# Moving the input rows and the two buffers of the normalised operand by 96 bytes within SBUF, in a two-block transformer layer

## The chip, the cores and the metric

The kernel runs on one core of one Trainium2 chip. The metric is the device time of one execution, in microseconds. Before the change three runs gave a median of 949.74 us (949.6 to 950.62).

## The reference

Two blocks of a layer model, one after the other, on 256 tokens of width 1024, all in float32:

```
h = rmsnorm(x, norm_mix)                               # norm 0
proj = h @ w_in                                        # state space, 3 attentions, gates
...
x = x + sum_i(sigmoid(gate_i) * (y_i @ w_branch_i)) @ w_out
h = rmsnorm(x, norm_ffn)                               # norm 1
x = x + (silu(h @ w_gate) * (h @ w_up)) @ w_down       # width 2816
x = rmsnorm(x, norm_final)
u = rms(x, ln_mix)                                     # norm 2
p = u @ w_in_2                                         # RWKV, latent attention, gated delta rule
...
x = x + y @ w_out_2
u = rms(x, ln_ffn)                                     # norm 3
x = x + relu(u @ w_ff1)**2 @ w_ff2                     # width 4096
```

## The kernel before

All weights stream from HBM through a ring of three slots of 16 KB per partition (`weights0` to `weights2`), in chunks of mostly 128 x 4096 values, fetched by SP's queue.

Products with the large weights are made with three matmuls in place of one. Each weight piece of 2048 columns is split into two parts: ScalarE copies it to a rounded part (`W_HIGH`, L1685), and VectorE subtracts that from the original (`W_LOW`, L2260). The other operand is split in the same way. `product3` (L680 to L688) then issues, for each tile of 128 rows of the contraction, high x high, high x low and low x high into the same accumulator. Its matmul is L686, and it is the line of most of TensorE's work. Every matmul has a weight load of its own: 128 columns of the stationary operand are loaded while the matmul before it streams its moving operand.

Two shapes occur at L686:

- 256 moving columns: the weight piece is stationary (`W_HIGH`, `W_LOW`), and the normalised operand, transposed, moves, all 256 tokens of it. The projections in of the first block read it from `FIRST_HIGH` and `FIRST_LOW` (over `BIAS`), those of the second block from `IN2_HIGH` and `IN2_LOW` (in `ARENA`), and both feed-forward parts, `ffn1` (11 chunks) and `ffn2` (8 chunks), from `OVER_HT` and `OVER_HN`. These two are names over the buffers `HT` and `HN`. A chunk is two jobs of `f_job_split` (L690), and a job two outputs of 8 x 3 matmuls: 11 x 2 x 2 x 24 = 1056 for `ffn1` and 8 x 2 x 2 x 24 = 768 for `ffn2`.
- 512 moving columns: the weights move and the operand is stationary (`t_half`, L710, the branch products and both `down` products). The stationary operand is mostly in `ARENA` or `BIAS`, for `out1` and a part of `out2` it is `OVER_HT` or `OVER_HN`. The last pieces of the `down` products and one piece of `branch` lie in `HT` and `HN` as moving weights.

Some chunks of `in2` are not split: L643 multiplies `HT` (moving) by the ring slot (stationary) in plain float32.

All engines' programs are written out by hand, each with its waits on semaphores. Places in SBUF come from the order of the allocations at the head of `build` (L239 to L258). `sb` takes the next free place, `placed` does so and also keeps it (they all begin on multiples of 32 bytes), and `over` lays a second name on a kept place. Sizes per partition: `X`, `HN` and `HT` 8192 bytes each, `STAT` 256, `RELB` 64 (on 32 partitions), `PICK0` 32, three ring slots of 16384, `BIAS` 16384, then `ARENA` with 104448. The offsets within `ARENA` of the pieces and of `IN2_HIGH`, `HID1_HIGH` and the like are multiples of 128 values, which is 512 bytes, and so are the steps between the tiles in them. So the modulo 512 of `ARENA`'s address is that of the ring slots, of `BIAS` and of all operands in them. There are two exceptions. `KEY_HIGH` and `KEY_LOW`, the second piece of the first `in2` chunk, have rows of 160 values, so that each further tile of the contraction starts 640 bytes on, 128 more modulo 512. `PICK0` and `PICK1` are tiny selectors, of which one column is repeated over all columns of an operand.

Of the kernel before, what the change touches and what calls it, by code (L numbers as in the profile page):

```python
# [20 lines left out]
ACT = mybir.ActivationFunctionType  # L21
AX_X = mybir.AxisListType.X

P = 128
# [5 lines left out]
NH = 8  # L30
# [183 lines left out]
def build(nc, x, weights, params, params2, consts, tables, rel_bias, norm_final, positions, table_dram, out):  # L214
    with ExitStack() as ctx:
        def sb(name, shape, dt=F32):
            return ctx.enter_context(nc.sbuf_tensor(name, shape, dt))
# [3 lines left out]
        def sem(name):  # L221

            if name not in sems:
                sems[name] = ctx.enter_context(nc.semaphore(name))
            return sems[name]
# [4 lines left out]
        def placed(name, shape):  # L230

            places[name] = (nc.sbuf_base + 31) // 32 * 32
            return sb(name, shape)

        def over(name, place, at, shape):

            return nc.alloc_sbuf_tensor_at(name, [P] + shape, F32R, offset=places[place] + 4 * at)

        X = sb("X", [P, TT, D])  # L239
        HN = placed("HN", [P, TT, D])  # L240
        HT = placed("HT", [P, KD, S])
        STAT = sb("STAT", [P, 64])
        RELB = sb("RELB", [32, 2 * NH])
        PICK = [placed("PICK0", [P, NH])]
        rings = [placed(f"weights{i}", [P, SLOT]) for i in range(NRING)]
        RING_LOW = [over(f"RING_LOW{i}", f"weights{i}", 0, [SLOT]) for i in range(NRING)]
        BIAS = placed("BIAS", [P, 16, S])
# [6 lines left out]
        PRM = sb("PRM", [P, NP1])  # L254
        PICK.append(placed("PICK1", [P, NH]))
        PICK = [over(f"PICK_PARTS{i}", f"PICK{i}", 0, [NH]) for i in range(2)]
        POS = sb("POS", [P, TT], I32)
# [59 lines left out]
        def tbl(name):  # L317
            a, b = TCOL[name]
            return TBL[:, a:b]
# [210 lines left out]
        def _(sp):  # L530
# [23 lines left out]
            for b in range(3):  # L554
                wait_fill_out(sp, ("down2", b))
                tt, dc = divmod(b, 2)
                sp.dma_start(out[0, tt * P:(tt + 1) * P, dc * 512:(dc + 1) * 512],
                             X[:, tt, dc * 512:(dc + 1) * 512]).then_inc(sem("out_stored"), 16)
            for j in range(2):
# [4 lines left out]
                cols = slice(512 + j * S, 512 + (j + 1) * S)  # L564
                sp.dma_start(out[0, P:S, cols], X[:, 1, cols]).then_inc(sem("out_stored"), 16)
            sp.wait_ge(sem("out_stored"), 16 * 5)
# [24 lines left out]
        def _(pe):  # L591
# [10 lines left out]
            def open_fill(name):  # L602
                f = state["fill"]
                assert FILLS[f][0] == name, (FILLS[f], name)
                b = FILLS[f][1]
                if FILL_USES[f]:
                    pe.wait_ge(sem(f"fill_out{b}"), FILL_USES[f])
                return BK[b]
# [9 lines left out]
            def close_fill(ins):  # L618
                state["fill"] += 1
                ins.then_inc(sem("fills_written"), 1)  # L620
# [154 lines left out]
            o = open_fill(("table",))  # L775
            close_fill(pe.matmul(o[0:2 * NH, 0:384], RELB[:, :], tbl("onehot")[0:32, :], start=True, stop=True))

# [33 lines left out]
            def both_parts(h, n, sign):  # L811

                return PICK[0 if sign > 0 else 1][:, h:h + 1].to_broadcast([P, n])

# [725 lines left out]
            def x_transposes(dc):  # L1540
# [3 lines left out]
                for b in (2 * dc, 2 * dc + 1):  # L1544
                    o = open_fill(("norm", 3, b))
                    for j in range(2):
                        for tt in range(TT):
                            k = 2 * b + j
                            ins = pe.transpose(o[:, j * S + tt * P:j * S + (tt + 1) * P],
                                               X[:, tt, k * P:(k + 1) * P], ident)  # L1550
                    close_fill(ins)
# [57 lines left out]
        def _(act):  # L1609
            for tt in range(TT):  # L1610
                act.dma_start(X[:, tt, :], x[0, tt * P:(tt + 1) * P, :]).then_inc(sem(f"x{tt}_in"), 16)
            act.dma_start(CST[:, 0:P], consts[:, 0:P]).then_inc(sem("params_in"), 16)
            act.dma_start(PRM[:, :], params).then_inc(sem("params_in"), 16)
            act.dma_start(TBL[0:32, :], tables).then_inc(sem("consts_in"), 16)
            act.dma_start(RELB[:, :], rel_bias).then_inc(sem("consts_in"), 16)
            act.dma_start(CST[:, P:NC], consts[:, P:NC]).then_inc(sem("consts_in"), 16)
# [9 lines left out]
            def half_squares(m, tt, dc):  # L1626
# [7 lines left out]
                else:  # L1634
                    wait_job_out(act, ("out1" if m == 1 else "out2", dc, tt))
                    junk = JUNK[m][:, 2 * tt + dc, :]
                cols = slice(dc * 512, (dc + 1) * 512)
                act.activation(junk, X[:, tt, cols], ACT.Square, accum_out=HALF_SUMS[:, 0, tt, dc:dc + 1])\
                    .then_inc(sem("half_sums"), 1)
# [567 lines left out]
        def _(dve):  # L2207
            steps = [0]

            def link(ins):  # L2210

                steps[0] += 1
                ins.then_inc(sem("dve_steps"), 1)
                dve.wait_ge(sem("dve_steps"), steps[0])
# [113 lines left out]
            link(dve.tensor_scalar(negident[:, :], ident, -1.0, None, ALU.mult))  # L2328
            dve.tensor_tensor(PICK[0][:, :], ident[:, 0:NH], ident[:, 32:32 + NH], ALU.add)
            dve.tensor_tensor(PICK[1][:, :], negident[:, 0:NH], negident[:, 32:32 + NH], ALU.add)  # L2330
            for tt in range(TT):
# [996 lines left out]
```

## Time and profile before

| | |
|---|---|
| median of 3 runs | 949.74 us (949.6 to 950.62) |
| profiled execution, its own time | 949.99 us |
| its span, first to last instruction | 948.4 us |
| TensorE busy, share of the span | 929.5 us, 98% |
| VectorE, ScalarE, GpSimd busy | 589.2, 470.8, 62.5 us |
| mean granted TensorE clock | 0.997 |
| moved by DMA | 149.86 MB |

The profiled execution took 0.25 us more than the median; its span leaves out 1.6 us around the instructions. A busy TensorE is not a TensorE at its peak, since matmuls overlap: a duration of one is not the time that it costs. What it costs is the distance from its start to the next one's start, called its interval below, and it is had from a stretch without waits, as time between the first and the last start divided by the number of matmuls less one.

### The profile page before, as it was taken

What the parts mean: (1) busy time and instruction counts of PE and PEld (TensorE: products, weight loads), DVE (VectorE), ACT (ScalarE), POOL (GpSimd) and SP (SyncE); (2) the same over time, 40 slices, a digit from 0 to 9 for tenths busy, and PEclk for the clock granted to TensorE, in tenths of its full rate; (3) what the DMA queues carried; (4) which work ended last, traced back from release to release, by engine and by line L of the source; (5) the groups of instructions that cost most, each with busy time, mean ns of one, the idle gap of its engine ahead of it and who ended that gap; (6) DMA issues with size and microseconds to landing.
All of it is one profiled execution on the core that took longest, in us unless ns stands there. A gap on an engine that the chain in (4) does not pass through costs nothing.

```text
span 948.4 us, 16840 instructions
## 1 busy us (share of the span) xinstructions
PE 929.5 (98%) x7117; PEld 825.9 (87%) x7117; DVE 589.2 (62%) x932; ACT 470.8 (50%) x707; POOL 62.5 (7%) x78
## 2 busy tenths in 40 slices
PE   6999999999999999999999999999999999999998
PEld 6999987787778789999988789888988799998886
DVE  5885445556678755555554669678867566655434
ACT  5654335555874454444443684556436454554331
POOL 1000000021003200000000000002450000000000
PEclk9999999999999999999999999999999999999999
DMA  9995552243446524445554442222000444555521
GB/s 349 205 375 192 189 189 89 90 167 131 164 188 250 191 107 178 178 178 188 189 200 162 178 148 100 89 90 90 3 2 18 163 178 178 189 188 205 214 94 45
DMA packets 14922, 149.86 MB, mean 158 GB/s; under 512 B 1712, under 2 KB 4144, under 8 KB 6272
## 3 DMA queue, kind: packets, MB, share of 16 engines
q1 hardware_dynamic: 12592, 139.65, 39.5%
q0 software_dynamic: 1296, 5.24, 3.0%
q10 hardware_dynamic: 960, 3.90, 1.1%
q8 instruction: 57, 0.93, 0.4%
q14 instruction: 17, 0.14, 0.0%
HBM read 144.59 MB, written 4.19 MB: 157 GB/s over the span
## 4 chain that ended last, share of the span: by engine, by line
PE 87%; DVE 5%; ACT 4%; issue 2%; POOL 1%; DMA 0%; ACTq 0%; DVEq 0%; POOLq 0%
PE bank L686 66%; PE bank L643 4%; PE bank L1423 3%; DVE W_LOW L2260 1%; PE bank L834 1%; POOL HN L3144 1%; PE bank L875 1%; PE bank L912 1%; ACT W_HIGH L1685 1%; PE bank L668 1%; PE bank L652 1%; PE bank L1290 1%; DMA PRM<-params_dram 0%; DVE OUT_LOW L2260 0%; DVE X L2567 0%
## 5 line engine op out<-in xcount | busy, mean ns | idle before, releaser
L2260 DVE TENSOR_TENSOR W_LOW<-weights,W_HIGH 128x2048 fp32r<-128x2048 f32 (+1 forms) x98 | 224.5, 2292 | 208.3 <-ACT W_HIGH L1685 208.2
L1685 ACT ACTIVATE W_HIGH<-weights 128x2048 fp32r<-128x2048 f32 (+1 forms) x98 | 186.7, 1907 | 257.0 <-PE bank L686 257.0
L686 PE MATMUL bank<-OVER_HT,W_HIGH 128*128 128x256 f32 x608 | 171.2, 282 | 0.2 <-DVE OVER_HN L2272 0.2
L686 PE MATMUL bank<-OVER_HT,W_LOW 128*128 128x256 f32 x608 | 170.7, 281 | 0.0
L686 PE MATMUL bank<-OVER_HN,W_HIGH 128*128 128x256 f32 x608 | 170.7, 281 | 0.0
L686 PEld LDWEIGHTS bank<-OVER_HT,W_HIGH 128*128 128x128 f32 x608 | 114.7, 189 | 0.8 <-issue 0.6
L686 PEld LDWEIGHTS bank<-OVER_HN,W_HIGH 128*128 128x128 f32 x608 | 114.6, 189 | 0.0
L686 PEld LDWEIGHTS bank<-OVER_HT,W_LOW 128*128 128x128 f32 x608 | 114.6, 189 | 0.0
L686 PE MATMUL bank<-W_LOW,HID_HIGH 128*128 128x512 f32 x200 | 77.9, 390 | 0.0
L686 PE MATMUL bank<-W_HIGH,HID_LOW 128*128 128x512 f32 x200 | 77.9, 390 | 0.0
L686 PE MATMUL bank<-W_HIGH,HID_HIGH 128*128 128x512 f32 x200 | 77.9, 390 | 0.0
L686 PE MATMUL bank<-FIRST_HIGH,W_HIGH 128*128 128x256 f32 x216 | 61.4, 284 | 0.0
L686 PE MATMUL bank<-FIRST_LOW,W_HIGH 128*128 128x256 f32 x216 | 61.2, 283 | 0.0
L686 PE MATMUL bank<-FIRST_HIGH,W_LOW 128*128 128x256 f32 x216 | 61.2, 283 | 0.0
L643 PE MATMUL bank<-HT,weights 128*128 128x256 f32 x240 | 55.4, 383 | 0.0
L686 PE MATMUL bank<-GATE_HIGH,FIRST_HIGH 128*128 128x512 f32 x128 | 52.4, 410 | 1.0 <-DVE RING_LOW L2401 1.0
L643 PEld LDWEIGHTS bank<-HT,weights 128*128 128x128 f32 x240 | 44.6, 190 | 6.5 <-issue 0.7
L686 PE MATMUL bank<-GATE_HIGH,FIRST_LOW 128*128 128x512 f32 x128 | 50.2, 392 | 0.0
L686 PE MATMUL bank<-RING_LOW,FIRST_HIGH 128*128 128x512 f32 x128 | 50.1, 391 | 0.0
L2401 DVE TENSOR_TENSOR RING_LOW<-weights,GATE_HIGH 128x1024 fp32r<-128x1024 f32 x32 | 40.7, 1271 | 11.8 <-ACT GATE_HIGH L1720 11.8
L686 PEld LDWEIGHTS bank<-W_LOW,HID_HIGH 128*128 128x128 f32 x200 | 37.6, 188 | 7.8
L686 PEld LDWEIGHTS bank<-W_HIGH,HID_LOW 128*128 128x128 f32 x200 | 37.6, 188 | 7.8
(523 smaller groups left out, 1868.4 us busy)
## 6 DMA issues: line engine op xcount, KB each, us to landing
weights<-weights_dram SPq DMA_DIRECT2D x63, 2048.0 KB, 7.9
bias_rows_dram<-ARENA POOLq DMA_DIRECT2D x1, 3072.0 KB, 39.1
weights<-weights_dram SPq DMA_DIRECT2D x2, 1024.0 KB, 5.9
BIAS<-params_dram ACTq DMA_DIRECT2D x1, 1997.0 KB, 13.9
weights<-weights_dram SPq DMA_DIRECT2D x1, 1664.0 KB, 6.8
weights<-weights_dram SPq DMA_DIRECT2D x1, 1584.0 KB, 6.9
X<-x_dram ACTq DMA_DIRECT2D x2, 512.0 KB, 4.3
HT<-bias_rows_dram POOLq DMA_DIRECT2D x1, 1024.0 KB, 8.7
```

The lines of the kernel that those rows point to most:

```text
L643: ins = pe.matmul(o, w[:, k, a:a + n], HT[:, k, :], start=(k == 0), stop=(k == KD - 1))
L652: pe.matmul(BK[j % 4][:, 0:P], ident, ident, start=True, stop=True)
L668: ins = pe.transpose(banks[b][:, j * S + tt * P:j * S + (tt + 1) * P], HN[:, tt, k * P:(k + 1) * P], ident)
L686: ins = pe.matmul(o, left[a][k], right[b][k], start=(first and k == 0 and a + b == 0), stop=(last and k == n - 1 and a == 1))
L834: ins = pe.matmul(BK[4 + u % 2][:, c0:c1], q[:, q0:q0 + P], k[:, 0:n], start=True, stop=(br != 2))
L875: ins = pe.transpose(probsT_bank(u)[:, j * P:(j + 1) * P], PB_[:, u % 2, j * P:(j + 1) * P], ident)
L912: ins = pe.matmul(o[pb:pb + HD, c0:S], V[:, n, a:a + HD], PT_[:, u % 2, k0:k1], start=(n == 0), stop=(n == 1))
L1290: ins = pe.matmul(o[pb:pb + HD, c * P:(c + 1) * P], a[:, c, h * HD:(h + 1) * HD], b[:, matrix(c, h), :], start=(n == 0), stop=(c == 0 and ...
L1423: ins = pe.matmul(o[b:b + HD, n * HD:(n + 1) * HD], left[b:b + HD, 4 * g + n, :], right[b:b + HD, 4 * g + n, :], start=True, stop=True)
L1685: act.activation(like_source(piece_parts(k)[0], k), piece_source(k), ACT.Copy).then_inc(sem("pieces_high"), 1)
L2260: dve.tensor_tensor(low, piece_source(k), high.bitcast(F32), ALU.subtract)\
L2401: dve.tensor_tensor(low, src, high.bitcast(F32), ALU.subtract).then_inc(sem("gate_split"), 1)
```

## The change

`RELB` and `PICK0` are allocated ahead of `X` in place of behind `STAT`. Nothing else differs: every engine has the same instructions in the same order, with the same waits.

```
+        RELB = sb("RELB", [32, 2 * NH])
+        PICK = [placed("PICK0", [P, NH])]
         X = sb("X", [P, TT, D])
         HN = placed("HN", [P, TT, D])
         HT = placed("HT", [P, KD, S])
         STAT = sb("STAT", [P, 64])
-        RELB = sb("RELB", [32, 2 * NH])
-        PICK = [placed("PICK0", [P, NH])]
         rings = [placed(f"weights{i}", [P, SLOT]) for i in range(NRING)]
```

`X`, `HN`, `HT` and `STAT` move up by 64 + 32 = 96 bytes; the ring slots and all that stands behind them stay. From `HT` to `ARENA` it was 8192 + 256 + 64 + 32 + 3 x 16384 + 16384 = 74080 bytes, which is 352 more than a multiple of 512 (144 x 512 = 73728); now it is 73984, which is 256 more. For `HN` and `X` it is the same modulo 512, since 8192 is a multiple of it. As a circle of 512 bytes, the operand in `HT` or `HN` stood 160 bytes from the pieces in `ARENA`, and now stands 256 from them. `FIRST_HIGH` and `IN2_HIGH` stand at distance 0 from the pieces, before and after.

## Rows read from the trace of the kernel before

**Rows 1.** The page, part 1: busy time of each engine.

```profile
PE 929.5 (98%) x7117; PEld 825.9 (87%) x7117; DVE 589.2 (62%) x932; ACT 470.8 (50%) x707; POOL 62.5 (7%) x78
```

**Rows 2.** The page, part 4: the chain that ended last, share by engine.

```profile
PE 87%; DVE 5%; ACT 4%; issue 2%; POOL 1%; DMA 0%; ACTq 0%; DVEq 0%; POOLq 0%
```

**Rows 3.** The chain in order of time: start, length (us), engine and line, matmuls.

```profile
353.11 185.51 PE bank L686 x1320
...
613.98 3.46 PE bank L643 x16
...
768.71 176.39 PE bank L686 x1140
```

**Rows 4.** What TensorE waited for: us in total, times, longest.

```profile
PE bank L668 <- DVE HN L2246: 8.7, 2, 8.5
```

**Rows 5.** Groups of instructions, shapes apart: busy us, mean ns of one.

```profile
L686 PE MATMUL bank<-OVER_HT,W_HIGH 128*128 128x256 f32 x608 | 171.2, 282 | 0.2 <-DVE OVER_HN L2272 0.2
...
L686 PE MATMUL bank<-FIRST_HIGH,W_HIGH 128*128 128x256 f32 x216 | 61.4, 284 | 0.0
...
L686 PEld LDWEIGHTS bank<-OVER_HN,W_HIGH 128*128 128x128 f32 x608 | 114.6, 189 | 0.0
...
L686 PEld LDWEIGHTS bank<-FIRST_LOW,W_HIGH 128*128 128x128 f32 x216 | 41.5, 192 | 0.0
```

**Rows 6.** L686 in 95:119, 400:440, 782:822, 885:925, 327:334: ns min/median/max, first, last start.

```profile
L686 PE MATMUL bank<-FIRST_HIGH,W_HIGH x68: 282/284/284, 94.7 to 118.8; 128*128 128x256 f32 x68
...
L686 PE MATMUL bank<-OVER_HN,W_HIGH x113: 276/282/283, 399.8 to 439.7; 128*128 128x256 f32 x113
...
L686 PE MATMUL bank<-OVER_HT,W_LOW x115: 277/280/283, 781.8 to 821.9; 128*128 128x256 f32 x115
...
L686 PE MATMUL bank<-W_HIGH,HID_HIGH x60: 388/390/390, 884.8 to 924.9; 128*128 128x512 f32 x60
...
L686 PE MATMUL bank<-W_HIGH,OVER_HT x11: 388/394/395, 326.7 to 333.6; 128*128 128x512 f32 x11
```

**Rows 7.** Busy us (instructions) of PE, PEld, DVE, ACT, POOL by stretch; clock, DMA share.

```profile
400.00:450.00 50.00, 50.00 (x424) 50.00 (x423) 28.19 (x21) 20.64 (x18) 0.00 (x0) 1.00 0.49 173
```

**Rows 8.** Matmuls in order of time: the KEY tiles, pieces with other offsets (start, length us).

```profile
551.25 0.28 PE L686 MATMUL bank<-IN_HIGH,KEY_HIGH 128*128 128x256 f32 x1
...
551.84 0.28 PE L686 MATMUL bank<-IN_HIGH,KEY_LOW 128*128 128x256 f32 x1
...
552.20 0.28 PE L686 MATMUL bank<-IN_HIGH,KEY_LOW 128*128 128x256 f32 x1
...
553.27 0.29 PE L686 MATMUL bank<-IN_HIGH,KEY_LOW 128*128 128x256 f32 x1
...
553.64 0.28 PE L686 MATMUL bank<-IN_HIGH,KEY_LOW 128*128 128x256 f32 x1
...
554.11 0.28 PE L686 MATMUL bank<-IN_HIGH,KEY_HIGH 128*32 128x256 f32 x1
...
554.80 0.28 PE L686 MATMUL bank<-IN_HIGH,KEY_HIGH 128*32 128x256 f32 x1
```

**Rows 9.** Products in which the repeated column of PICK moves: ns min/median/max, first and last start.

```profile
L851 PE MATMUL bank<-PICK_PARTS,DECAY_PARTS x16: 270/272/273, 177.3 to 201.4; 128*128 128x256 f32 x8, 128*128 128x128 f32 x8
```

**Rows 10.** Plain float32 products in order of time: L668 loads HN, L652 only CST.

```profile
542.99 1.04 PE L668 MATMUL bank<-CST,HN 128*128 128x128 f32 x8
543.87 1.28 PE L652 MATMUL bank<-CST 128*128 128x128 f32 x10
```

**Rows 11.** Instructions and DMAs that touch X: ns min/median/max, first and last start.

```profile
L2567 DVE SCALAR_TENSOR_TENSOR X<-bank,X x12: 681/684/692, 338.7 to 766.7; 128x512 f32<-128x512 f32 x12
...
DMA to landing us min/median/max: 1.7/2.0/4.9
```

More of the change, by code:

```diff
@@ L237, in over @@
             return nc.alloc_sbuf_tensor_at(name, [P] + shape, F32R, offset=places[place] + 4 * at)
+        RELB = sb("RELB", [32, 2 * NH])
+        PICK = [placed("PICK0", [P, NH])]
         X = sb("X", [P, TT, D])
@@ L242, in build @@
         STAT = sb("STAT", [P, 64])
-        RELB = sb("RELB", [32, 2 * NH])
-        PICK = [placed("PICK0", [P, NH])]
         rings = [placed(f"weights{i}", [P, SLOT]) for i in range(NRING)]
```

## The prediction, made before the result was known

> **What bounds the kernel now.** I read first the busy times, then the chain, then TensorE's waits, and last its matmuls by shape and place. The busy times show TensorE at 98% of the span [rows 1]. By itself that says little, since matmuls overlap. The chain confirms it: 87% of what ended last is TensorE [rows 2], and two pieces of it alone, of 185.51 us with 1320 matmuls and of 176.39 us with 1140, are L686 without a break [rows 3]. Its longest wait, 8.7 us in all, is for the first norm at the start [rows 4]. In such a stretch VectorE is busy 28.19 of 50 us, ScalarE 20.64, the DMA engines 0.49 of the time, and the granted clock is 1.00, its upper level of 2.4 GHz [rows 7]. So nothing holds TensorE there but its own pace, and a nanosecond on each matmul of L686 is a nanosecond of the kernel.
>
> That pace is not one number, and this is the clue for a change that moves addresses alone. The intervals of matmuls of one and the same shape [rows 6]:
>
> - moving FIRST, distance 0 from the pieces modulo 512: (118.8 - 94.7) us / (3 x 67) = 119.9 ns.
> - moving OVER_HT and OVER_HN, distance 160, ffn1: (439.7 - 399.8) / (3 x 112) = 118.75 ns.
> - the same in ffn2: (821.9 - 781.8) / (3 x 114) = 117.25 ns.
> - 512 moving columns, all at distance 0: (924.9 - 884.8) / (3 x 59) = 226.6 ns.
> - 512 moving columns, stationary OVER_HT or MIX_LOW: (333.6 - 326.7) / (3 x 10) = 230 ns.
>
> The weight loads differ too: 192 ns beside FIRST, 189 beside OVER_HT [rows 5]. A matmul therefore pays something to the load that runs beside it, and how much goes with where the two read. Two rows bound it from below. With one column of PICK repeated as the moving operand, a matmul takes 272 ns, and never over 273 [rows 9], where streaming ones take 280 to 284 [rows 6]. Duration less interval is 164.1, 163.3 and 162.8 ns in the three places above (284, 282 and 280 ns of duration), so 272 stands for an interval near 109 ns. And where only 32 columns are loaded, the interval is (554.80 - 554.11) / 6 = 115 ns [rows 8].
>
> **The change part by part.** It adds and removes no instruction. Three groups of accesses change their distance from 160 to 256.
>
> (a) 1056 + 768 = 1824 matmuls of ffn1 and ffn2, by far the most. No row has this pair at 256; the KEY tiles pass through 0, 128, 256 and 384, three loads at each, too few to settle. All 24 average (554.11 - 551.25) / 24 = 119 ns; those whose loads stand at 256 give (552.20 - 551.84) / 3 = 120 and (553.64 - 553.27) / 3 = 123 [rows 8]. The bounds per matmul are 109 (nothing paid) and 123. For the value I take the trend of the long stretches, which are nearest in kind: from distance 0 to 160 the interval falls by 1.15 ns (ffn1) and 2.65 ns (ffn2), and 256 is 1.6 times as far. That gives 118.06 and 115.66 ns, so 1056 x -0.69 = -0.73 us and 768 x -1.59 = -1.22 us, together -1.95 us. Why ffn1 and ffn2 differ at the same distance is not explained by any row. It is a warning that the modulo 512 is not all.
>
> (b) Matmuls with 512 columns in triples that touch HT or HN: out1 and out2 96 each, down 48, branch 24, together 264. They pay 3.4 ns more than those at distance 0 [rows 6]. By the same trend 5.4 at 256: 264 x 2.0 = +0.54 us. Bounds: back to 226.6, 264 x -3.4 = -0.9 us; twice the trend, +1.1 us.
>
> (c) 240 plain matmuls of L643, moving HT: 3.46 us for 16 [rows 3], 216 ns each, 51.9 us in all. The moving operand goes at half the pace here. The nearest rows to what an offset does to plain products are L668, (1.04 - 0.27) / 7 = 110 ns, and L652 with both operands at one place, (1.28 - 0.28) / 9 = 111 [rows 10]. That is 1%, so -0.5 to +0.5 us; I take 0.
>
> (d) VectorE, ScalarE and GpSimd on X, HN and STAT: the 12 updates of X take 681 to 692 ns [rows 11]. I cost their move at nothing, covered by TensorE's unbroken work. Without that cover 1% of 12 x 684 ns is 0.08 us. The DMAs of X land in 2.0 us in the median, 4.9 at most [rows 11]; only the first and the last are uncovered, and if a start within a row mattered by 5%, it would be 0.25 us. I take 0, since the same rows go to the same partitions. RELB and PICK0, small and early, get nothing.
>
> Sum: -1.95 + 0.54 = **-1.4 us** against the profiled execution of 949.99 us (span 948.4), which stands 0.25 us above the median of the runs. From the median: 949.74 - 1.4 = **948.3 us**.
>
> A rule of the Trainium skill speaks against any effect. SBUF — State Buffer, "Who interferes with whom", gives TensorE two independent read ports, one for the moving operand and one for weight loads; TensorE: Matmul & The Clock Gate, "Step-by-step: what each phase is for", concludes that loading the next weights steals nothing from the running matmul. By that rule (a) to (c) are 0 and the time stays 949.7 us. The trace does not bear it out in full: 119.9 and 117.25 ns for one shape. The second page's "Back-to-back issue gap" puts an isolated matmul of 256 columns at columns / 2.4 + 2.5, 109.2 ns as an estimate, so a full removal would be worth some 16 us by it; the 272 ns of the selector row points to the same floor.
>
> **The rivals.**
>
> 1. The two reads part for good. If the cost comes from both streams meeting in the same part of memory, half the circle may be where they never do, and the interval falls to between 115 and 109. For: 272 ns against 280 to 284 shows that there are some 10 ns to gain. Against: 160 is far already and freed only 1 to 3 ns, and no KEY triple near 256 was quick. At 115: 3.75 x 1056 + 2.25 x 768 = 5.7 us, so 944.0; at 109.5: 9.8 + 6.0 = 15.7 us, so 934.0. A middle of 112 gives 938.5 us.
>
> 2. It goes by a smaller modulo. Distance 256 is 0 modulo 256, 128 and 64, where 160 is not. If that is the rule, HT now stands as FIRST does: 119.9 ns. 1.15 x 1056 + 2.65 x 768 = +3.25 us, with (b) giving back 0.9: 952.1 us, **slower**. For: nothing in long stretches excludes it. Against: the KEY tiles move by multiples of 128 only, and their triples go from 120 to 123 and others below, where this rival wants them all alike. It decides from 1 ns per matmul up.
>
> 3. The meeting falls in the middle of the load and costs most there. A moving operand goes at twice the pace of the load and so comes round to it once per matmul wherever it starts; at distance 0 that is at the edge. 120 and 123 ns for the two KEY triples at 256 point to it. At 123: 4.25 x 1056 + 5.75 x 768 = 8.9 us, 958.6 us.
>
> 4. The distance does not matter: the places differ by something else, as ffn1 and ffn2 do, or the change does nothing by the ports' rule. 949.7 us.
>
> **How the numbers follow.** A measurement of this kernel tells about 0.2%, 1.9 us, from no change. The forecast, a small shift in either direction around -1.4 us, has 0.40, of which 0.18 is faster by over 0.2%, 0.20 within it and 0.02 slower. Rival 1 has 0.24, all faster, with the shallow half the likelier. Rival 2 has 0.14 and rival 3 has 0.09, all slower. Rival 4 has 0.13, all within. Faster: 0.42; within: 0.20 + 0.13 = 0.33; slower: 0.14 + 0.09 + 0.02 = 0.25. The forecast's own range is 946 to 950.5. For 8 in 10 it must reach into rival 1, to 939 (its deep half, 0.12, stays out), and over rival 2 with part of rival 3, to 954.
>
> **What would show it.** In the profile after, the stretches of ffn1 and ffn2 must hold the whole difference: an interval near 118.1 and 115.7 ns if I am right, 109 to 115 with durations near 273 for rival 1, 119.9 with weight loads of 192 ns for rival 2, above 121 for rival 3. The matmuls moving FIRST must stay at 119.9, those of the down products at 226.6; if these moved as well, distance to ARENA is not the cause. The out1 stretch shows (b), 16 matmuls of L643 in other than 3.46 us would show (c). Waits of TensorE should be the same; a new one, or a first norm wait other than 8.5 us, would put a part outside my account.

## The result and the profile after

| | before | after |
|---|---|---|
| median, us | 950.18 (949.6 to 952.66, 8 runs) | 953.66 (952.07 to 954.48, 8 runs) |
| ratio | | 1.003, 95% interval 1.0018 to 1.0041 |
| profiled execution, us | 949.99, span 948.4 | 953.59, span 952.0 |
| TensorE busy, us | 929.5 | 933.2 |

The changed kernel is slower by some 3.5 us, where the forecast was 1.4 us faster. The time lies inside the predicted range, on the side of rival 2, whose working gave 952.1 us from the median of 949.74.

The first view of the profile after is L686 in the same five stretches as [rows 6] (minimum, median and maximum duration in ns, first and last start in us):

```profile
L686 PE MATMUL bank<-FIRST_HIGH,W_LOW x68: 283/283/284, 94.8 to 118.9; 128*128 128x256 f32 x68
...
L686 PE MATMUL bank<-OVER_HT,W_HIGH x112: 283/283/284, 399.7 to 439.7; 128*128 128x256 f32 x112
...
L686 PE MATMUL bank<-OVER_HT,W_HIGH x112: 283/283/284, 781.8 to 821.7; 128*128 128x256 f32 x112
...
L686 PE MATMUL bank<-W_LOW,HID_HIGH x60: 389/389/389, 884.7 to 924.8; 128*128 128x512 f32 x60
...
L686 PE MATMUL bank<-W_HIGH,OVER_HT x11: 389/389/476, 327.1 to 334.0; 128*128 128x512 f32 x11
```

Read them as [rows 6] were read, as time from first to last start over the number of starts between. FIRST, which did not move, has (118.9 - 94.8) / (3 x 67) = 119.9 ns, as before. ffn1 has (439.7 - 399.7) / (3 x 111) = 120.1 ns in place of 118.75, and ffn2 (821.7 - 781.8) / (3 x 111) = 119.8 in place of 117.25. Both long stages now go as FIRST goes. So do the spreads: 276 to 283 ns of duration before, 283 to 284 now, every matmul alike. The 512 columns beside HID are unchanged at 226.6 ns. Those beside OVER_HT had durations of 388/394/395 and now have a median of 389, that of the undisturbed ones. The first of them, 476 ns long, stands behind a pause of 1 us; from the window's second triple on, the trace's starts are 226.8 ns apart, and 231.1 before.

The costliest groups of the page say it again. The 608 matmuls of a kind took 282 ns in the mean before [rows 5] and take 284 now, and the weight loads beside them rose from 189 to 192 ns, the number of FIRST's loads in [rows 5]:

```profile
L686 PE MATMUL bank<-OVER_HT,W_HIGH 128*128 128x256 f32 x608 | 172.6, 284 | 0.3 <-DVE OVER_HN L2272 0.3
...
L686 PEld LDWEIGHTS bank<-OVER_HN,W_HIGH 128*128 128x128 f32 x608 | 116.7, 192 | 0.0
```

Where the time went, in the chain of work that ended last (start us, us, what), next to [rows 3]:

```profile
12.16 2.45 PE bank L652 x12
...
23.46 26.11 PE bank L686 x216
...
354.09 186.76 PE bank L686 x1320
...
616.20 3.46 PE bank L643 x16
...
770.50 178.17 PE bank L686 x1140
```

The piece with ffn1 grew from 185.51 to 186.76 us, the one with ffn2 from 176.39 to 178.17: 3.03 us. What lies between the stage at 23.46 and the piece with ffn1, and between the two pieces, shrank by 0.26 and 0.44 us: there lie most of the 512-column matmuls that touch HT and HN. The plain products of L643 take 3.46 us as they did. The other 1.24 us of this pair of executions is in the start, before anything of L686. The chain of before has there

```profile
22.22 26.10 PE bank L686 x216
```

and so the same stage, 1.24 us earlier. The stretch from 11.8 to 14.4 us, in the kernel before and in the changed one:

```profile
11.80:14.40 2.60, 2.60 (x26) 2.60 (x24) 2.60 (x7) 2.60 (x7) 2.00 (x1) 1.00 1.15 423
```

```profile
11.80:14.40 2.60, 2.60 (x15) 2.60 (x13) 2.60 (x7) 2.60 (x7) 2.03 (x1) 1.00 1.13 419
```

The number in the first brackets is the matmuls of these 2.6 us: 26 before, 15 now. The same matmuls of L652 start 213 ns apart here and 111 ns apart before. The clock column says 1.00 in both rows, but the trace's first record of the granted clock begins only at 14.4 us here and at 11.8 us before, and the pace doubles just there. That it is the lower level of 1.2 GHz that ends there is an inference. In the kernels below that first record begins at 12.6 to 13.8 us, whatever their layout, so this differs between executions, and it is not counted for the change. The sum is closed: 1.24 + 3.03 - 0.26 - 0.44 = 3.57 of the 3.6 us between the spans. So the two long stages and what lies between them are worth 3.03 - 0.70 = 2.33 us, while the medians lie 3.5 us apart.

A part of the rest is the granted clock once more, this time on record. Both profiled executions have one stretch of 3.4 us at the lower level, between the two long pieces (before, then changed; the third number from the end is the granted share of 2.4 GHz):

```profile
687.60:691.00 3.40, 3.40 (x57) 3.38 (x57) 2.28 (x6) 1.89 (x7) 1.33 (x2) 0.50 0.00 0
```

```profile
690.20:693.60 3.40, 3.40 (x56) 3.40 (x49) 2.46 (x6) 2.32 (x7) 2.03 (x3) 0.50 0.00 0
```

TensorE was busy without a pause before both falls. Not every execution has the stretch, and the mean clock of an execution tells: near 0.998 with 3.4 us of it, 0.996 with 6.8 us, 1.000 with none. The changed kernel took 952.07 and 952.26 us in its two executions at 1.000, and 953.36 to 954.48 in its six at 0.998. In the comparisons below, before took 950.0 us in the mean of its 31 executions at 1.000. Like with like the change costs 2.1 us, close to the 2.33 of the chain, though two executions are few.

TensorE's waits are those of [rows 4]:

```profile
PE bank L668 <- DVE HN L2246: 8.7, 2, 8.5
```

So the place is where the prediction said it would be, and the direction is not.

### The profile page after: what moved, and what is told of

Read it like the earlier page. It is cut to its first block, busy times and chain, and to the rows that moved or that the text cites. A ratio compares the mean times of both kernels' runs of the same rounds, so it can differ in the third digit from the quotient of the medians.

```text
span 952.0 us, 16840 instructions
## 1 busy us (share of the span) xinstructions
PE 933.2 (98%) x7117; PEld 830.1 (87%) x7117; DVE 588.7 (62%) x932; ACT 470.8 (49%) x707; POOL 62.4 (7%) x78
## 4 chain that ended last, share of the span: by engine, by line
PE 87%; DVE 5%; ACT 4%; issue 2%; POOL 1%; DMA 0%; ACTq 0%; DVEq 0%; POOLq 0%
PE bank L686 66%; PE bank L643 4%; PE bank L1423 3%; DVE W_LOW L2260 1%; PE bank L834 1%; POOL HN L3144 1%; PE bank L875 1%; PE bank L912 1%; ACT W_HIGH L1685 1%; PE bank L652 1%; PE bank L668 1%; PE bank L1290 1%; DMA PRM<-params_dram 0%; DVE OUT_LOW L2260 0%; PE bank L1184 0%
## 5 line engine op out<-in xcount | busy, mean ns | idle before, releaser
L686 PE MATMUL bank<-OVER_HT,W_HIGH 128*128 128x256 f32 x608 | 172.6, 284 | 0.3 <-DVE OVER_HN L2272 0.3
L686 PE MATMUL bank<-OVER_HN,W_HIGH 128*128 128x256 f32 x608 | 172.1, 283 | 0.0
L686 PE MATMUL bank<-OVER_HT,W_LOW 128*128 128x256 f32 x608 | 172.1, 283 | 0.0
L686 PEld LDWEIGHTS bank<-OVER_HT,W_HIGH 128*128 128x128 f32 x608 | 116.7, 192 | 0.9 <-issue 0.7
L686 PEld LDWEIGHTS bank<-OVER_HN,W_HIGH 128*128 128x128 f32 x608 | 116.7, 192 | 0.0
L686 PEld LDWEIGHTS bank<-OVER_HT,W_LOW 128*128 128x128 f32 x608 | 116.7, 192 | 0.0
L686 PE MATMUL bank<-W_LOW,HID_HIGH 128*128 128x512 f32 x200 | 77.8, 389 | 0.0
L686 PE MATMUL bank<-W_HIGH,HID_HIGH 128*128 128x512 f32 x200 | 77.8, 389 | 0.0
L686 PE MATMUL bank<-W_HIGH,HID_LOW 128*128 128x512 f32 x200 | 77.8, 389 | 0.0
L686 PE MATMUL bank<-FIRST_HIGH,W_HIGH 128*128 128x256 f32 x216 | 61.3, 284 | 0.0
L686 PE MATMUL bank<-FIRST_HIGH,W_LOW 128*128 128x256 f32 x216 | 61.1, 283 | 0.0
L686 PE MATMUL bank<-FIRST_LOW,W_HIGH 128*128 128x256 f32 x216 | 61.1, 283 | 0.0
L643 PE MATMUL bank<-HT,weights 128*128 128x256 f32 x240 | 55.4, 383 | 0.0
L686 PE MATMUL bank<-GATE_HIGH,FIRST_HIGH 128*128 128x512 f32 x128 | 52.4, 409 | 1.0 <-DVE RING_LOW L2401 1.0
L643 PEld LDWEIGHTS bank<-HT,weights 128*128 128x128 f32 x240 | 44.5, 190 | 6.6 <-issue 0.7
L686 PE MATMUL bank<-GATE_HIGH,FIRST_LOW 128*128 128x512 f32 x128 | 50.2, 392 | 0.0
L686 PE MATMUL bank<-RING_LOW,FIRST_HIGH 128*128 128x512 f32 x128 | 50.0, 391 | 0.0
L2401 DVE TENSOR_TENSOR RING_LOW<-weights,GATE_HIGH 128x1024 fp32r<-128x1024 f32 x32 | 40.6, 1270 | 11.8 <-ACT GATE_HIGH L1720 11.8
L686 PEld LDWEIGHTS bank<-W_HIGH,HID_HIGH 128*128 128x128 f32 x200 | 37.6, 188 | 7.8
L686 PEld LDWEIGHTS bank<-W_LOW,HID_HIGH 128*128 128x128 f32 x200 | 37.6, 188 | 7.8
## 6 DMA issues: line engine op xcount, KB each, us to landing
BIAS<-params_dram ACTq DMA_DIRECT2D x1, 1997.0 KB, 13.8
```

The lines of the kernel that those rows point to most:

```text
L643: ins = pe.matmul(o, w[:, k, a:a + n], HT[:, k, :], start=(k == 0), stop=(k == KD - 1))
L686: ins = pe.matmul(o, left[a][k], right[b][k], start=(first and k == 0 and a + b == 0), stop=(last and k == n - 1 and a == 1))
L2401: dve.tensor_tensor(low, src, high.bitcast(F32), ALU.subtract).then_inc(sem("gate_split"), 1)
```

## The experiments

These theories stood at the start. T256: the cost goes by the distance modulo 256. T128 and T64: a period of 128 or 64; rival 2 had named all three. T512: modulo 512, as the forecast's trend and rival 3 have it. Tabs: not the distance but the absolute address of the operand. "Distance" is throughout the operand's address less that of the weight piece, in bytes. With 256 columns the operand moves and the piece is stationary, with 512 columns it is the other way round.

### TensorE alone, the whole circle

A kernel with TensorE alone, on tiles of zeros, that leaves out all of the reference's computation: 48 matmuls of 256 columns for each distance (192 in the first stretch), in the order high by high, high by low, low by high, against pieces at the kernel's own places.

```diff
+ TESTS = [("wide", d, "A") for d in (160, *range(0, 512, 32))]
...
+ w, m = pieces[name], views[k]
+ for n in range(8):
+     for a, b in ((0, 0), (0, 1), (1, 0)):
+         pe.matmul(o[:, 0:256], w[a][:, n, t % 2 * P:(t % 2 + 1) * P], m, ...)
```

> Nothing of the layer is computed: TensorE alone runs the three-matmul pattern on zeros, one stretch of 48 (256 moving columns), 24 (512) or 8 (plain float32) matmuls for each distance of the moving from the stationary operand, modulo 512. T64 (what counts is the distance modulo 64): 256-column intervals of 120 ns at distances 0, 64, 128, ... 448, and of 117 to 119 at 32, 96, ... 480. T128 or T256: 120 only at multiples of 128 or 256. T512 (my forecast's trend): 120 at 0, falling towards 256. Tabs (the moving operand's own address modulo 64): as T64 here, since the stationary pieces stay at 480 modulo 512, but 256-column intervals at distances of 4 to 24 would then all be the same. For pieces B (ffn2's place) the same by all. 512-column rows: 226.7 where the 256-column ones give 120, 231 elsewhere. If it takes the whole layer's traffic to make the difference, all distances give one interval.

Mean intervals in ns after the first few, worked out from the starts in the trace:

| distance | 0 | 32 | 64 | 96 | 128 | 160 | 192 | 224 |
|---|---|---|---|---|---|---|---|---|
| d | 120.0 | 116.6 | 117.8 | 120.0 | 118.6 | 117.4 | 113.3 | 118.3 |
| d + 256 | 119.9 | 116.7 | 117.8 | 120.0 | 120.0 | 117.3 | 113.3 | 118.3 |

The rows of six of these tiles (same columns as above; the maximum is the first matmul after a wait):

```profile
L70 PE MATMUL bank<-AT0wideA,WH_A x32: 276/283/388, 47.9 to 53.5; 128*128 128x256 f32 x32
...
L70 PE MATMUL bank<-AT256wideA,WH_A x32: 280/283/387, 96.7 to 102.3; 128*128 128x256 f32 x32
...
L70 PE MATMUL bank<-AT64wideA,WH_A x32: 277/279/388, 60.1 to 65.6; 128*128 128x256 f32 x32
...
L70 PE MATMUL bank<-AT320wideA,WH_A x32: 278/279/388, 109.0 to 114.5; 128*128 128x256 f32 x32
...
L70 PE MATMUL bank<-AT192wideA,WH_A x32: 276/276/387, 84.7 to 90.0; 128*128 128x256 f32 x32
...
L70 PE MATMUL bank<-AT448wideA,WH_A x32: 276/276/386, 133.6 to 138.9; 128*128 128x256 f32 x32
```

The two rows of the table are the same circle twice, but for 128 against 384. The change moved the operand from 160 (117.4) to 256 (119.9), the same as 0. T512 falls with it, since 0 and 256 are alike, and T64, since 64 differs from 0. T128 falls by 96 and 224: 120.0 in both rows against 118.3. Eight distances against ffn2's pieces gave the same numbers, but for 160 with 118.7. Small distances speak against Tabs, which wants them alike: 123.3, 116.7, 118.7 and 120.0 ns at 4, 8, 16 and 24 bytes. The curve is not smooth either. Between 160 and 256 lies 192 with 113.3, the best of all, so no straight line through two of its points could have told a third.

With 512 moving columns the distances 0 and 256 give 226.6 and 226.7 ns, the five others measured (32, 64, 96, 160, 352) 233 to 234.4; plain float32 matmuls give 215.8 ns at 0, at 160 and at 256:

```profile
L76 PE MATMUL bank<-WH_A,AT256longA x16: 388/389/499, 268.2 to 273.6; 128*128 128x512 f32 x16
...
L76 PE MATMUL bank<-WH_A,AT160longA x16: 392/398/499, 262.2 to 267.6; 128*128 128x512 f32 x16
```

So 0 modulo 256 is the best place at 512 columns and near the worst at 256.

And one distance could have two paces. The first, long stretch at 160 went at 118.8 ns, a later one at 117.4: the two numbers that ffn2 and ffn1 had in the whole kernel (117.25 and 118.75) with places swapped. In each stretch the intervals, uneven at first, fall after 5 to 10 matmuls into a cycle that repeats to within a nanosecond.

### The whole kernel, by 96 bytes everywhere

```diff
+        sb("PAD", [P, 24])
         X = sb("X", [P, TT, D])
```

> 96 unused bytes ahead of X: everything moves by 96, the distance of HT from ARENA stays 160 as before, HT stands at 224 modulo 512 as after the change. All theories of distance: ffn1 at 118.7 ns per matmul, ffn2 at 117.3, the first block's projections (FIRST) at 119.9, time that of before, 949.7 to 950.2 us. Tabs: ffn1 and ffn2 at 120.0 (HT is now 32 off a multiple of 64), FIRST at 117 to 119 (BIAS now on a multiple of 64): 3 us more and 1 us less.

950.34 us (948.32 to 952.49, 10 runs), ratio 1.0001 (0.9988 to 1.0014): no change. The operand's absolute address is now the one of the changed kernel, 96 bytes on, and its pace is not, and FIRST, moved too, stays at 120.0: Tabs falls. The rows of ffn1 and ffn2 (L687 is L686):

```profile
L687 PE MATMUL bank<-OVER_HT,W_LOW x115: 277/280/282, 399.8 to 439.9; 128*128 128x256 f32 x115
...
L687 PE MATMUL bank<-OVER_HN,W_HIGH x114: 277/281/283, 781.7 to 822.0; 128*128 128x256 f32 x114
```

The rows give 117.25 and 118.9 ns, the trace's starts 117.3 and 118.7: the two paces of distance 160, and against before they have changed places. What the prediction noted as unexplained, that ffn1 and ffn2 differ at one distance, was no property of the stages.

### Distance 224 and distance 192 in the whole kernel

One of the two small tiles alone ahead of X, where the change puts both:

```diff
+        RELB = sb("RELB", [32, 2 * NH])
         X = sb("X", [P, TT, D])
...
-        RELB = sb("RELB", [32, 2 * NH])
```

> RELB alone ahead of X: X, HN and HT move by 64 bytes, distance 224. T64, T128 and T256: no multiple of 64, so ffn1 and ffn2 stay near 118.7 and 117.3 ns, time as before within 1.5 us. T512: nearly the full way to 256 and so nearly the change's result, 120 ns and 953 us.

950.84 us (950.14 to 952.15), ratio 1.0002 (0.9991 to 1.0013). Both long stages at (439.9 - 399.8) / (3 x 113) = 118.3 ns, what TensorE alone gave at 224:

```profile
L686 PE MATMUL bank<-OVER_HT,W_HIGH x114: 277/281/285, 399.8 to 439.9; 128*128 128x256 f32 x114
```

And PICK0 alone in the same way:

> PICK0 alone ahead of X: X, HN and HT move by 32 bytes, distance 192. T64: 120.0 ns in ffn1 and ffn2, weight loads of 192 ns, out1 at 227 in place of 231, time as after the change, 952 to 954 us. T128 and T256: as before, 118.7 and 117.3 ns, 950 us. T512: between the two.

946.05 us (941.66 to 950.05, 7 runs), ratio 0.9949 (0.9922 to 0.9975): faster, by the third of the change that moves the operand 32 bytes only. No theory had put this kernel below before, T256 neither: a period alone tells nothing of the places inside it. The spread is the widest of all the kernels, and the profiled execution was one of the longest (949.78), at 117.7 ns in both stages:

```profile
L686 PE MATMUL bank<-OVER_HT,W_HIGH x114: 281/281/281, 399.8 to 439.7; 128*128 128x256 f32 x114
```

TensorE alone had 113.3 ns here. The difference from 117.8, the trace's number for both stages, is 8.2 us on 1824 matmuls, about the distance between the longest and the shortest execution, 8.4 us.

### TensorE alone again: finer steps, unequal distances, openings

> TensorE alone on zeros: stretches of 48 matmuls of 256 columns in the order of the long stages (high by high, high by low, low by high), each after a wait, with 0 to 7 short matmuls of 64 columns ahead of it. Scanned: the distance in steps of 4 bytes from 176 to 236 modulo 256, the distance 192 with seven different openings, and all pairs of different distances of the high and the low moving part in steps of 32 bytes. Theory PATTERNS (a weight load and the moving reads meet with a period of 256 bytes, the starts lock into a repeating cycle, and which cycle depends also on how the stretch begins): distance 192 gives 113.3 ns after some openings and 118.0 ns after others, with nothing in between that lasts; pairs lie between 113 and 123 ns. Theory DISTANCE ALONE: distance 192 gives 113.3 ns after every opening, and the whole kernel's 118.0 ns came from other traffic in its memory. Either would show a pair or a distance that stays below 115 ns if there is one; mine is that the best stays near 113 ns, above the 106.7 ns that 256 columns take at one a cycle of 2.4 GHz.

An opening is what stands ahead of a stretch: here a number of short matmuls of 64 columns. Distances in steps of 4 bytes, after two openings (0 and 3 short matmuls), intervals in ns:

| 176 | 180 | 184 | 188 | 192 | 196 | 200 | 204 |
|---|---|---|---|---|---|---|---|
| 119.3 / 119.3 | 123.3 / 120.0 | 120.0 / 120.0 | 115.6 / 115.6 | 113.3 / 113.3 | 120.0 / 120.0 | 120.0 / 120.0 | 116.7 / 116.7 |

| 208 | 212 | 216 | 220 | 224 | 228 | 232 | 236 |
|---|---|---|---|---|---|---|---|
| 119.2 / 116.7 | 120.1 / 120.1 | 121.3 / 121.3 | 116.7 / 116.7 | 118.4 / 118.3 | 120.0 / 120.2 | 120.0 / 119.8 | 115.6 / 115.6 |

Four bytes beside the best distance, at 196, it is 120.0 ns. Among all 56 pairs of unequal distances of the high and the low part none was under 116.9, and none over 120.0. At 192 six openings of eight gave 113.3 and two 117.8, nothing between: PATTERNS holds, DISTANCE ALONE falls. The run that counts the openings came later, after the miss told below:

> TensorE alone on zeros: 48 matmuls of 256 columns at the distances 188, 192, 160, 0 and 32 (modulo 256), each after a wait and with 0 to 9 matmuls of 64 or of 256 columns ahead of the stretch. PATTERNS: one distance has a few cycles and the opening picks one of them: 192 gives 113.3 or about 118 ns and 160 gives 117.4 or 118.8 ns; 188 has, besides the 115.6 ns of the run before, the slower cycle that the whole kernel stayed in (118.7 ns by its first stage), in some openings; 0 gives 120.0 ns after nearly every opening, since both long stages and the first stage of the whole kernels never left it. OTHER TRAFFIC (what VectorE, ScalarE and the DMA do in the whole kernel makes the slower rows at 188): 188 gives 115.6 ns after all 20 openings.

It has 0 to 9 matmuls ahead of each stretch, of 64 or of 256 columns. How many of the 20 openings led to which cycle:

| distance | cycles, ns |
|---|---|
| 0 | 120.0 in 20 |
| 32 | 116.7 in 17, 117.8 in 3 |
| 160 | 117.3 in 13, 118.7 in 6, 120.0 in 1 |
| 188 | 115.6 in 5, 120.0 in 15 |
| 192 | 113.3 in 14, 117.8 in 6 |

Two stretches at 192 and two at 188, each inside its cycle:

```profile
L68 PE MATMUL bank<-AT192wide,WH_A x23: 276/276/276, 174.2 to 178.0; 128*128 128x256 f32 x23
```

```profile
L68 PE MATMUL bank<-AT192wide,WH_A x24: 281/281/281, 198.9 to 202.9; 128*128 128x256 f32 x24
```

```profile
L68 PE MATMUL bank<-AT188wide,WH_A x20: 276/276/277, 52.9 to 56.1; 128*128 128x256 f32 x20
...
L68 PE MATMUL bank<-AT188wide,WL_A x11: 277/277/277, 52.7 to 56.2; 128*128 128x256 f32 x11
```

```profile
L68 PE MATMUL bank<-AT188wide,WH_A x14: 282/282/282, 60.0 to 62.2; 128*128 128x256 f32 x14
```

One kernel, one distance, the same 48 instructions: 276 or 281 ns to the last matmul at 192, 276 or 282 at 188. An opening doesn't fix it for good either: distance 160 with no short matmul ahead gave 118.7 once and 117.3 another time within this run. The ten openings with matmuls of 256 columns led to the longer cycle more often, 10 times at 188 and 5 at 192, than the ten with short ones, 5 times and once. Of these five distances only 0 has a single cycle, and that is what the change chose. It fits that no execution of the changed kernel was under 952.07 us, while before had executions down to 948.03 in the comparisons of this study; what spread the changed kernel has left, 952.07 to 954.48, goes with the granted clock, as shown above.

### The period, in the whole kernel

```diff
+        STAT = sb("STAT", [P, 64])
         X = sb("X", [P, TT, D])
...
-        STAT = sb("STAT", [P, 64])
```

> STAT (256 bytes) is placed ahead of the input rows, so X, HN and HT move by 256 bytes and nothing behind them moves: the distance of the long stages goes from 160 to 416 modulo 512. Theory PERIOD 256: 160 and 416 are the same to the memory, so the long stages keep one of the two cycles of distance 160 (117.4 or 118.8 ns), OVER_HT at 512 columns stays at 231 ns, and the time is 950.2 us within 1.5 us. Theory PERIOD 512 with another symmetry (the distance counted one way, low at 416): 1824 matmuls near 113 to 115 ns, 943 to 947 us; or if 256 apart were special by itself, 120.0 ns and 953.5 us.

950.65 us (948.11 to 951.46, 10 runs), ratio 0.9991 (0.998 to 1.0002), before at 951.08 in the same comparison. 256 bytes on, nothing changed: 117.25 ns in ffn1 and 118.75 in ffn2, the two cycles of 160.

```profile
L686 PE MATMUL bank<-OVER_HT,W_LOW x115: 277/280/282, 399.8 to 439.9; 128*128 128x256 f32 x115
...
L686 PE MATMUL bank<-OVER_HN,W_HIGH x113: 277/281/283, 781.8 to 821.7; 128*128 128x256 f32 x113
```

T256 predicted this, and neither form of T512 that was written down did.

### X alone

```diff
+        RELB = sb("RELB", [32, 2 * NH])
+        PICK = [placed("PICK0", [P, NH])]
         X = sb("X", [P, TT, D])
+        sb("GAP0", [P, 40])
         HN = placed("HN", [P, TT, D])
         HT = placed("HT", [P, KD, S])
+        sb("GAP1", [P, 24])
...
-        RELB = sb("RELB", [32, 2 * NH])
-        PICK = [placed("PICK0", [P, NH])]
```

> The part of the change that moves X, alone: RELB and PICK0 ahead of the input rows, so X moves by 96 bytes as in the change, and a gap of 160 bytes behind X, so that HN and HT stand at 416 from the pieces, which is 160 modulo 256; a gap of 96 bytes behind HT keeps the arena. If the long stages' operand is the whole cause, the time is that of before, 950.2 to 951.1 us (within 1.5), and L686 stays at 117 to 119 ns; if X's place costs or gives anything, it shows beyond that. The rival, that all of the change's loss belongs to X and STAT, gives 953.7 us.

950.73 us (948.46 to 953.08, 10 runs), ratio 1.0003 (0.9989 to 1.0017), 118.75 ns in both stages:

```profile
L688 PE MATMUL bank<-OVER_HT,W_HIGH x113: 277/281/283, 399.8 to 439.7; 128*128 128x256 f32 x113
```

The part of the change that moves X by 96 bytes, and RELB and PICK0 with it, costs nothing beyond the interval of -1.0 to +1.6 us; the operand's part is all that shows.

### A better place, and a miss

The first stage never left 120.0 ns either, since its operand stands at 0. Its tile gets 64 elements more (256 bytes, so the arena keeps its place modulo 256), and it starts 48 elements (192 bytes) on; PICK0 stands ahead of X:

```diff
-        BIAS = placed("BIAS", [P, 16, S])
+        BIAS = placed("BIAS", [P, 16 * S + 64])
...
+        FIRST = over("FIRST", "BIAS", 0, [16 * S + 64])
+        FIRST_HIGH, FIRST_LOW = [FIRST[:, 48 + i * KD * S:48 + (i + 1) * KD * S].rearrange("p (k s) -> p k s", k=KD)
+                                 for i in range(2)]
...
```

> As distance 192 (PICK0 ahead of the input rows), and the operand of the first stage (FIRST_HIGH, FIRST_LOW, in the place of BIAS) moves by 192 bytes as well, with 256 bytes more behind its start so that the arena keeps its place modulo 256. PATTERNS: the first stage's 648 matmuls go from 120.0 ns to 118.0 or 113.3 ns, so 1.3 to 4.3 us less than the 946.05 us of distance 192 alone: median 941.8 to 944.8 us, fastest near 937 us where all three stages fall into the 113.3 ns cycle, slowest near 949 us. DISTANCE ALONE (no choice of cycle) would give one time for all executions. If what moves FIRST does not count, 946 us.

942.84 us (939.19 to 946.96, 6 runs), ratio 0.9925 (0.9906 to 0.9944), as the patterns predict. The profiled execution is the 939.19 us one, with all three stages in the short cycle (L688 is L686; the shift is two lines):

```profile
L688 PE MATMUL bank<-FIRST,W_HIGH x133: 276/276/276, 94.7 to 117.2; 128*128 128x256 f32 x133
```

```profile
L688 PE MATMUL bank<-OVER_HT,W_LOW x119: 276/276/276, 399.8 to 439.9; 128*128 128x256 f32 x119
```

```profile
L688 PE MATMUL bank<-OVER_HT,W_HIGH x119: 276/276/276, 781.8 to 822.0; 128*128 128x256 f32 x119
```

(439.9 - 399.8) / (3 x 118) = 113.3 ns, 119 matmuls where before fitted 113. In its chain the two pieces take

```profile
351.23 180.01 PE bank L688 x1320
...
760.83 173.45 PE bank L688 x1140
```

that is 5.50 and 2.94 us less than [rows 3], where 1056 x 5.45 = 5.8 and 768 x 3.95 = 3.0 were to be had. Not all of FIRST's move is gain: its 144 matmuls with 512 columns went from 227 to 229 ns, since they leave distance 0.

The fourth stage's operand moved within the arena, and RATES behind it:

```diff
-        IN2_HIGH, IN2_LOW = over("IN2_HIGH", "ARENA", 11008, [KD, S]), over("IN2_LOW", "ARENA", 13056, [KD, S])
+        IN2_HIGH, IN2_LOW = over("IN2_HIGH", "ARENA", 11056, [KD, S]), over("IN2_LOW", "ARENA", 13104, [KD, S])
...
-        RATES_HIGH, RATES_LOW = over("RATES_HIGH", "ARENA", 15104, [KD, 40]), over("RATES_LOW", "ARENA", 15424, [KD, 40])
+        RATES_HIGH, RATES_LOW = over("RATES_HIGH", "ARENA", 15152, [KD, 40]), over("RATES_LOW", "ARENA", 15472, [KD, 40])
```

> As w5 (distance 192 in the first stage and in both long ones), and the operand of the fourth stage, IN2_HIGH and IN2_LOW, moves by 192 bytes within the arena as well (RATES_HIGH and RATES_LOW behind it too). PATTERNS: its 256-column matmuls go from 120.0 ns to 118.0 or 113.3 ns; they are some 110 in the stretch 560 to 575 us and about twice that in all, so 0.4 to 1.5 us less than the 942.84 us of w5: 941.3 to 942.6 us at the median, with single executions from 937 to 947. If the fourth stage is held by something else, 942.8 us.

942.91 us (941.08 to 947.53, 6 runs), ratio 0.992 (0.9896 to 0.9943), where 941.3 to 942.6 was expected. The stage did leave 283 ns, for the longer cycle of 281; against the kernel above nothing can be told, for the choice of cycles in the long stages outweighs it. Here ffn1 sat in the one cycle and ffn2 in the other, in a single execution:

```profile
L688 PE MATMUL bank<-OVER_HT,W_LOW x114: 281/281/281, 399.7 to 439.7; 128*128 128x256 f32 x114
```

```profile
L688 PE MATMUL bank<-OVER_HT,W_HIGH x119: 276/276/276, 781.8 to 821.9; 128*128 128x256 f32 x119
```

The miss came from distance 188, which after two openings had looked nearly as good (115.6 ns) and steadier. HN and HT became one tile read from its eighth element on:

```diff
-        HN = placed("HN", [P, TT, D])
-        HT = placed("HT", [P, KD, S])
+        WIDE = placed("HN", [P, 2 * KD * S + 64])
+        places["HT"] = places["HN"] + 4 * KD * S
+        HN, HT = [WIDE[:, 7 + i * KD * S:7 + (i + 1) * KD * S].rearrange("p (k s) -> p k s", k=k)
+                  for i, k in enumerate((TT, KD))]
...
```

> HN and HT become one tile of 64 elements more, read from its eighth element on: distance 188 modulo 256 from the pieces in the long stages; the first stage's operand at 188 too; the four pieces that lie in HT or HN stand at the hidden tiles' distance (0). PATTERNS: at 188 both openings of the run of TensorE alone gave the one cycle of 115.6 ns, so 1824 x 2.4 ns = 4.4 us against 950.2 us in the long stages (118.0 ns mean there) and 648 x 4.4 = 2.9 us in the first, 0.3 us from the moved pieces: 942.7 us, with a smaller spread than at 192. DISTANCE ALONE gives the same number. If matmuls that read from an address that is no multiple of 32 bytes, or the writes into it by VectorE and ScalarE, cost more in the whole kernel, it is above 946 us, and the rows of L686 or of the copies show it.

951.53 us (951.18 to 952.92, 11 runs), ratio 1.0011 (1.0002 to 1.0021): 8.8 us off, and level with before.

```profile
L692 PE MATMUL bank<-OVER,W_LOW x114: 277/278/282, 399.7 to 439.9; 128*128 128x256 f32 x114
```

(439.9 - 399.7) / (3 x 113) = 118.6 ns in place of 115.6. VectorE's and ScalarE's rows did not grow (588.2 and 470.9 us busy), so the unaligned operand itself costs them nothing. Two openings had been too few: of 20, as the table above shows, 15 lead to another cycle. But that one is 120.0 ns, and the kernel's is 118.6, an uneven cycle of 115 to 123 ns that TensorE alone never showed at 188. What selects it in the whole kernel stays open.

## Why the prediction was wrong, point by point

**What bounds the kernel** held: a nanosecond on each matmul of L686 is a nanosecond of the kernel. The two long pieces of the chain grew by 3.03 us, where the growth of the intervals, 1.15 ns on 1056 and 2.65 on 768 matmuls, makes 3.25.

**Term (a), -1.95 us, is the step that failed.** It took "the trend of the long stretches" from distance 0 to 160 and carried it on to 256, as if distance modulo 512 were a quantity with a slope. The runs show a period of 256 bytes, so that 256 is 0, and within it a curve that goes 120.0, 116.6, 117.8, 120.0, 118.6, 117.4, 113.3, 118.3 in steps of 32. The term measured +3.03 us in the chain, where its rival put +3.25. The text had the number that should have replaced the trend in its first list: 119.9 ns for FIRST, whose distance is 0. The modulo 512 came from the way in which the change was described and not from a row. No row excluded 256, and a candidate period that turns the new value into one already measured has a price from a row; a straight line has none. The median lies 1.6 us above rival 2's 952.1. The chain's +2.33 us agrees with rival 2's sum of +2.35; for the rest the clock is the likely cause, since the two executions without a stretch at the lower level took 952.2 us in the mean.

**The argument against rival 2 failed as well.** It held that the KEY triples, at multiples of 128, would all be alike if 256 were the period. But a pace needs 5 to 10 matmuls to settle, so three loads per distance showed transients [rows 8]. By the table, 0 and 128 need not be alike either. The same transients had been the support of rival 3, 123 ns, which nothing at 256 bore out.

**Term (b), +0.54 us, had the wrong sign for the same reason.** The 512-column matmuls at 0 modulo 256 go at 226.7 ns; the stretches around the long pieces shrank by 0.70 us, near the bound of -0.9 that the term had for the return to that pace. Its 230 ns for out1 was a rounding: the row's starts have one decimal, and by the trace it was 231.1.

**Term (c), 0, was right**: 3.46 us for 16 as before, and TensorE alone has 215.8 ns at three distances. **Term (d), 0, was right** for X within 1.6 us, by the kernel with X alone.

**The floor of 109 ns**, from which rival 1 had its prices, rested on a row that cannot carry it: of the 16 matmuls of [rows 9] eight have 128 columns and eight 256, and all last 270 to 273 ns, so their duration does not tell the interval of 256 columns. No run had a steady cycle under 113.3 ns.

**"Why ffn1 and ffn2 differ at the same distance is not explained"** was the best clue and was used as a warning only. The two numbers are two cycles of distance 160, they change places between kernels with the same distances, and TensorE alone shows both.

**The rules of the Trainium skill** that spoke against any effect are not borne out for these split matmuls; for the plain float32 ones, 215.8 ns at three distances, the trace agrees with them. SBUF — State Buffer, "Who interferes with whom", has independent read ports for the moving operand and the weight loads; the runs have 113.3 to 123.3 ns for one shape, by nothing but the distance between the two and the opening. That they meet in the memory is an inference from this, since no row shows the memory itself. TensorE: Matmul & The Clock Gate, "Back-to-back issue gap", gives for an isolated matmul of 256 columns, and not for a stream with weight loads, 109.2 ns as an estimate; the lowest cycle of any run here, all with a load per matmul, was 113.3.

**The chances.** Rival 2 had 0.14 and was right in place, sign and pace (119.9 and loads of 192 ns), and in its sum; which of its three periods it was, it left open. That the time came to lie inside the stated range is due to the range, which was drawn to take in rival 2, and not to the forecast. No row that held spoke for the period 512 over 256, so it should have had about as much as the forecast.

## What to carry to other kernels

Where a change moves only addresses, look for a stretch that already stands at the new distance modulo each smaller power of two; its pace is a better forecast than any trend. Before believing the pace of a short stretch, see whether its intervals repeat, and count several executions and openings: a distance with two cycles can win or lose 4% of a matmul by chance. Here the operands of the split matmuls with 256 columns are best at 192 bytes modulo 256 from their pieces (942.8 against 951.1 us), and those with 512 columns at 0. Compare the mean clock of the executions as well: a few us at the lower level can be as much as the change.

## What the runs showed of the hardware that was not expected

- The pace of back-to-back matmuls that each load new weights depends on the distance between what is loaded and what moves, with a period of 256 bytes: 113.3 to 123.3 ns at 256 columns, 226.6 to 234.4 at 512. Plain float32 matmuls, 215.8 ns, don't feel it.
- The pace locks into exactly repeating cycles, and one distance can have several (117.3, 118.7 and 120.0 ns at 160; 113.3 and 117.8 at 192). Which one it is differs between executions and within one. A part of the spread of this kernel's times is that choice.
- Another part is the granted clock: some executions have 3.4 or 6.8 us at 1.2 GHz near 690 us, with TensorE busy before it as in those that have none. In the changed kernel, with its single cycle, 3.4 us of it go with 1.1 to 2.4 us of time.
- Four bytes count: 192 gives 113.3 ns and 196 gives 120.0.
- The best distance for 256 columns is not the best for 512: at 192 the latter went at 229 ns in the whole kernel, at 0 at 226.7, and 0 is near the worst for 256.
